# A tenth place for a piece of expert weights, and the spill branch ahead of the last scatter

## The chip, the cores and the metric

The kernel runs on one core of a Trainium2 chip. The metric is device microseconds for one execution; before the change three runs gave 1014.17, 1015.07 and 1015.34 us, a median of 1015.07. TensorE is called PE, VectorE DVE, ScalarE ACT, GpSimd POOL and SyncE SP, as in the profile.

## The reference

Two transformer blocks follow each other on 256 tokens of width 1024, all in float32. Only the end of the first and the start of the second matter here: a mixture of 32 experts (two of them per token, each a SwiGLU with three matrices of 2 MB), a norm with the gain `norm_final`, and then the second block's projections.

```python
def hierarchical_moe(h, w_rg, b_rg, w_re, b_re, w_gate, w_up, w_down):
    ...
    def expert_rows(args):
        xb, e = args
        g = xb @ w_gate[e]
        u = xb @ w_up[e]
        return (jax.nn.silu(g) * u) @ w_down[e]
    ...
# the end of first_block, then the start of second_block
x = x + hierarchical_moe(rms_norm(x, norm_ffn[l]), ...)
return rms_norm(x, norm_final)
...
u = rms_norm_2(h, norm_mix_pre[layer])
u = moba_attention(u, attn_w_qkv[j], attn_w_o[j])
```

## The kernel before, in words

**The ring.** SBUF holds a ring of nine places (`RING`), each a piece of 2 MB: one of the matrices gate, up or down of one expert. Expert n (counted from 0) has the three places from `slots_of(n)` = (6 + 3n) mod 9 on, so expert n takes the places of expert n-3. In the first block the same memory holds other weights; experts 0 and 1 are loaded while that block ends (L592 to L600), and expert 2's three pieces as soon as it has ended.

**The loads.** SP alone issues the weights, in the order of its program, on one queue. `expert_loads` (L1650) first waits until PE has done `gate_up` of expert n-3 and issues gate and up, then waits for `down` of expert n-3 and issues down. Expert 3 has its own form, `expert_three` (L1719): its gate and up come in four quarters each, as expert 0's are used up, and its down piece after `down` of expert 0.

**The steps.** For each expert PE does `gate_up` (L1519, 32 matmuls), the turn of the hidden rows (L1530) and `down` (L1541, 16 matmuls); between them stand gathers of the next three experts' tokens (L1493), and after every second expert the scatter of a pair (L1552). ACT makes the silu and the high part of the result (L1584), DVE the product and the low part (L1644). Each expert has 64 slots for tokens. Experts 1 to 6 are written out, the rest run in a hardware loop of six experts per round, and expert 31's step stands behind it (L1803).

**After the loop.** SP waits for `gate_up` and `down` of expert 29 and issues the first six units of the second block's weights, 1 MB each, into places 3, 4 and 5 (L1824); after `gate_up` of expert 30 it issues the seventh and eighth, into place 6. These units are v0.0, v0.1, q0, k0, q1, k1, q2 and k2. Every engine then loads the flag that tells whether some expert has more than 64 tokens (L1833). PE does the last scatter (L1834), and only then does `nc.If(spill > 0)` (L1886, in the profile under L1817) branch over the program for such tokens, which isn't run with these inputs.

**The second block's start.** ACT takes squares of the scattered sums from PSUM (L2085). DVE waits for the last scatter and for the row `norm_final` (L2315, L2316) and multiplies the sums by it (L2234, `z_gained`); then come means, the scaled rows (L2247), PE's transposes (L484) and the first products (L433 to L435). The row was loaded long before, in the first block (L587), into `bc` ("gain_rows"), a tile of its own of 4 KB per partition; later gain rows come into the same tile.

Of the kernel before, what the change touches and what calls it, by code (L numbers as in the profile page):

```python
# [5 lines left out]
F32 = mybir.dt.float32  # L6
# [151 lines left out]
def build_program(nc, a, out):  # L158
# [41 lines left out]
    bc = nc.alloc_sbuf_tensor("gain_rows", [P, 1024], F32)  # L200
# [8 lines left out]
    spill_flag = nc.alloc_sbuf_tensor("spill_flag", [1, 1], I32)  # L209
    banks = [nc.alloc_psum_tensor(f"bank{i}", [P, 512], F32) for i in range(8)]  # L210
# [13 lines left out]
    def weight_parts(name, offset):  # L224
        return [[rounded(f"{name}_{part}{i}", UNIT, offset + (2 * i + k) * TILE)
                 for k, part in enumerate(("high", "low"))] for i in range(2)]

    LANE_SLOTS = (7, 0, 1, 6)
    lanes1, parts1 = pieces(*LANE_SLOTS), weight_parts("w1", slot_at(3))
    parts1.append([rounded("w1_high2", UNIT, arena_at + 4 * TILE), rounded("w1_low2", UNIT, LOW1)])  # L230
    lanes2, parts2 = pieces(3, 4, 5, 6), weight_parts("w2", slot_at(0))
# [331 lines left out]
    def first_sync():  # L563
# [22 lines left out]
        SP.wait_ge(*vgain.at(1))  # L586
        load_row("norm_final", a["norm_final"].rearrange("(l n) -> l n", l=1))  # L587
# [945 lines left out]
    def down(q, n, w, odd):  # L1533
# [3 lines left out]
        wd = ring[:, w * PIECE:(w + 1) * PIECE].rearrange("p (c n) -> p c n", n=D)  # L1537
# [8 lines left out]
    def scatter(q, y_made, turned_, b, h, signal):  # L1546
# [3 lines left out]
        for t in range(JT):  # L1550
            for y in Y[t]:
                last = PE.matmul(ACC[2 * h + t][:, :], ROUTET[:, b, t, h, :], y[:, :], start=False, stop=True,  # L1552
                                 skip_group_check=True)
        if signal:
            last.then_inc(*q.inc("scattered"))
# [94 lines left out]
    def expert_loads(q, e, n, w, w_dn, sems, gate_up_read=None):  # L1650
        if gate_up_read is not None:
            SP.wait_ge(*q.at("gate_up", gate_up_read))
        for i, src in enumerate((w_gate, w_up)):
            SP.dma_start(ring[:, (w + i) * PIECE:(w + i + 1) * PIECE],
                         src[bass.ds(e, 1), :, :].rearrange("o p n -> (o p) n")).then_inc(sems[i], 16)
        SP.wait_ge(*q.at("down", n))
        SP.dma_start(ring[:, w_dn * PIECE:(w_dn + 1) * PIECE],
                     w_down[bass.ds(e, 1), :, :].rearrange("o p n -> (o p) n")).then_inc(sems[2], 16)

    def slots_of(n):  # L1660
        return (6 + 3 * n) % RING
# [162 lines left out]
    for u in order2[0:6]:  # L1824
        load_second(u)
# [620 lines left out]
```

## Time and profile before

| | |
|---|---|
| median of the three runs | 1015.07 us |
| the profiled execution's own time | 1013.95 us |
| its span | 1012.7 us |
| mean granted clock of TensorE | 0.986 |
| DMA traffic | 289.66 MB, of which the experts' weights 201 MB |
| PE, DVE, ACT busy | 94%, 44%, 36% |

The span is shown on the page as 40 slices of 25.3 us each. The experts run in slices 10 to 28, from some 243 to 701 us. Times in the trace are us from the start of the span. In the view of the chain that ended last, "issue" is time for which the profile shows no releaser; in the DMA view, the last number of an issue is the time from its issue on SP to its landing.

### The profile page before, as it was taken

What the parts mean: (1) busy time and instruction counts of PE and PEld (TensorE: products, weight loads), DVE (VectorE), ACT (ScalarE), POOL (GpSimd) and SP (SyncE); (2) the same over time, 40 slices, a digit from 0 to 9 for tenths busy, and PEclk for the clock granted to TensorE, in tenths of its full rate; (3) what the DMA queues carried; (4) which work ended last, traced back from release to release, by engine and by line L of the source; (5) the groups of instructions that cost most, each with busy time, mean ns of one, the idle gap of its engine ahead of it and who ended that gap; (6) DMA issues with size and microseconds to landing.
All of it is one profiled execution on the core that took longest, in us unless ns stands there. A gap on an engine that the chain in (4) does not pass through costs nothing.

```text
span 1012.7 us, 13539 instructions
## 1 busy us (share of the span) xinstructions
PE 956.6 (94%) x5353; PEld 653.8 (65%) x5353; DVE 441.1 (44%) x757; ACT 360.3 (36%) x593; POOL 26.2 (3%) x40
## 2 busy tenths in 40 slices
PE   6999989998999999999999999985999989999997
PEld 5979878985444444444444444332998879998886
DVE  5856555445232232222222222214564755555434
ACT  7635446433121121111111112114455544554332
POOL 1400000000000000000000000000000000000000
PEclk9989999998999999999999999999999989999999
DMA  9943443486899999999999999999645535555501
GB/s 319 361 146 126 167 164 134 161 316 264 311 430 421 429 428 426 427 429 428 429 428 430 428 428 428 428 428 362 212 156 165 167 107 164 180 192 172 205 1 42
DMA packets 72629, 289.66 MB, mean 286 GB/s; under 512 B 4993, under 2 KB 44545, under 8 KB 60546
## 3 DMA queue, kind: packets, MB, share of 16 engines
q1 hardware_dynamic: 72002, 288.79, 73.8%
q8 instruction: 35, 0.57, 0.2%
q10 hardware_dynamic: 576, 0.17, 0.1%
q14 instruction: 16, 0.13, 0.0%
HBM read 287.90 MB, written 1.05 MB: 285 GB/s over the span
## 4 chain that ended last, share of the span: by engine, by line
PE 79%; issue 6%; ACT 6%; DVE 5%; DMA 4%; POOL 1%; SPq 0%; ACTq 0%; DVEq 0%
PE bank L1519 21%; PE bank L433 11%; PE bank L434 11%; PE bank L435 11%; PE bank L1541 10%; PE bank L1493 4%; DMA ring<-in_w_up 3%; ACT w_high L494 3%; PE bank L1552 3%; DVE w_low L523 1%; DVE arena L2303 1%; PE bank L1530 1%; ACT hidden_high L2127 1%; PE bank L723 1%; PE bank L761 1%
## 5 line engine op out<-in xcount | busy, mean ns | idle before, releaser
L1519 PE MATMUL bank<-ring,arena 128*64 128x512 f32 x1024 | 228.7, 598 | 7.9 <-issue 7.1
L523 DVE TENSOR_TENSOR w_low<-ring,w_high 128x2048 fp32r<-128x2048 f32 x76 | 174.1, 2290 | 122.3 <-ACT w_high L494 122.3
L494 ACT ACTIVATE w_high<-ring 128x2048 fp32r<-128x2048 f32 x76 | 145.1, 1909 | 120.8 <-PE bank L435 120.7
L1519 PEld LDWEIGHTS bank<-ring,arena 128*64 128x64 f32 x1024 | 75.5, 137 | 140.9 <-issue 139.0
L1541 PE MATMUL bank<-ring,arena 128*64 128x512 f32 x512 | 116.9, 597 | 5.3 <-issue 5.3
L433 PE MATMUL bank<-xT_high,w_high 128*128 128x256 f32 x384 | 112.0, 292 | 2.6 <-DVE xT_low L532 1.8
L434 PE MATMUL bank<-xT_low,w_high 128*128 128x256 f32 x384 | 109.8, 286 | 0.0
L435 PE MATMUL bank<-xT_high,w_low 128*128 128x256 f32 x384 | 109.7, 286 | 0.0
L1644 DVE SCALAR_TENSOR_TENSOR y_low<-bank,arena,y_high 64x512 fp32r<-64x512 f32 x64 | 48.0, 750 | 139.3 <-ACT y_high L1584 138.8
L1584 ACT ACTIVATE y_high<-bank,arena 64x512 fp32r<-64x512 f32 x64 | 43.7, 683 | 135.3 <-PE bank L1541 134.9
L1571 ACT ACTIVATE arena<-bank 128x256 f32<-128x256 f32 x32 | 12.3, 385 | 191.1 <-PE bank L1519 191.1
L1541 PEld LDWEIGHTS bank<-ring,arena 128*64 128x64 f32 x512 | 37.4, 136 | 63.3 <-issue 63.3
L433 PEld LDWEIGHTS bank<-xT_high,w_high 128*128 128x128 f32 x384 | 74.8, 195 | 4.4 <-issue 2.0
L1638 DVE TENSOR_TENSOR arena<-bank,arena 128x256 f32<-128x256 f32 x32 | 13.6, 424 | 146.2 <-ACT arena L1571 146.2
L434 PEld LDWEIGHTS bank<-xT_low,w_high 128*128 128x128 f32 x384 | 74.8, 195 | 0.1
L435 PEld LDWEIGHTS bank<-xT_high,w_low 128*128 128x128 f32 x384 | 74.8, 195 | 0.0
L1493 PEld LDWEIGHTS bank<-onehot,rows_high 128*128 128x128 f32 x176 | 34.6, 197 | 31.7 <-issue 31.5
L433 PE MATMUL bank<-w_high,hidden_high 128*128 128x512 f32 x128 | 50.0, 391 | 0.7 <-DVE arena L2303 0.5
L435 PE MATMUL bank<-w_high,hidden_low 128*128 128x512 f32 x128 | 49.8, 389 | 0.0
L434 PE MATMUL bank<-w_low,hidden_high 128*128 128x512 f32 x128 | 49.8, 389 | 0.0
L1493 PE MATMUL bank<-onehot,rows_high 128*128 128x192 f32 x176 | 46.0, 298 | 1.0 <-DVE onehot L1593 1.0
L1493 PE MATMUL bank<-onehot,rows_low 128*128 128x192 f32 x176 | 43.0, 280 | 0.0
(280 smaller groups left out, 1455.9 us busy)
## 6 DMA issues: line engine op xcount, KB each, us to landing
ring<-in_w_down SPq DMA_DIRECT2D x32, 2048.0 KB, 25.0
ring<-in_w_gate SPq DMA_DIRECT2D x31, 2048.0 KB, 21.3
ring<-in_w_up SPq DMA_DIRECT2D x31, 2048.0 KB, 25.8
ring<-in_w_up SPq DMA_DIRECT2D x16, 1024.0 KB, 5.6
ring<-in_w_down SPq DMA_DIRECT2D x16, 1024.0 KB, 5.0
ring<-in_attn_w_qkv SPq DMA_DIRECT2D x12, 1024.0 KB, 11.8
ring<-in_w_in SPq DMA_DIRECT2D x10, 1024.0 KB, 11.7
ring<-in_w_kv_mem SPq DMA_DIRECT2D x8, 1024.0 KB, 5.2
```

What stands on the lines that cost most here:

```text
L433: PE.matmul(o, lh, rh, start=start, stop=False, skip_group_check=True)
L434: PE.matmul(o, lh, rl, start=False, stop=False, skip_group_check=True)
L435: return PE.matmul(o, ll, rh, start=False, stop=stop, skip_group_check=True)
L494: SC.activation(parts[buffer[0][u]][0][:, :], lanes[n % len(lanes)], ACT.Copy).then_inc(*high.inc(u))
L523: DVE.tensor_tensor(p[1][:, :], lanes[n % len(lanes)], p[0][:, :].bitcast(F32), ALU.subtract).then_inc(*split.inc(u))
L1493: last = PE.matmul(bank[:, c * width:(c + 1) * width], part[:, h, k * P:(k + 1) * P], ONEHOT[buffer][:, h, 0:width], start=h == 0 and part ...
L1519: last = PE.matmul(GU[t * SLOTS:(t + 1) * SLOTS, 0:NGU], xs[:, k, :], wgu[:, :, k, t * (DE // JT):(t + 1) * (DE // JT)], start=k == 0, sto ...
L1541: last = PE.matmul(DN[t * SLOTS:(t + 1) * SLOTS, 0:NY], HT[:, o:o + SLOTS], wd[:, k, (t ^ odd) * NY:((t ^ odd) + 1) * NY], start=k == 0, s ...
L1552: last = PE.matmul(ACC[2 * h + t][:, :], ROUTET[:, b, t, h, :], y[:, :], start=False, stop=True, skip_group_check=True)
L1584: last = SC.activation(Y[t][0][p, :], DN[p, 0:NY], ACT.Copy, scale=SLOT_WEIGHT[p, b, t:t + 1])
L1638: DVE.tensor_tensor(HID, GU[:, DE // JT:NGU], SILU, ALU.mult).then_inc(*q.inc("hidden"))
L1644: last = DVE.scalar_tensor_tensor(out=Y[t][1][p, :], in0=DN[p, 0:NY], scalar=SLOT_WEIGHT[p, b, t:t + 1], in1=Y[t][0][p, :].bitcast(F32), o ...
```

## The change

A tenth place, `extra`, is allocated; its first 4 KB per partition are the tile `bc`, which has no memory of its own any more. Only one piece goes there: expert 3's down. It needs no place of expert 0 and is issued right after the quarters of gate and up. From expert 4 on all places are lower by one: expert 4 has up in place 8 (where expert 0's down was), gate in 1 and down in 0; expert 5 has 2, 3, 4; expert 6 has 5, 6, 7; expert 7 again 1, 8, 0. So in experts 4 to 6 one piece is issued after `down` of expert n-4 and the two others after `gate_up` of expert n-3. From expert 7 on each takes the places of expert n-3 and waits as before.

`norm_final` can't stay in `bc` while expert 3's down is there. Its load moves from the first block to behind the sixth unit of the second block's weights. Of those units four are issued after expert 29 (places 3 and 4), and the fifth and sixth, the row, the seventh and eighth after `gate_up` of expert 30.

The branch over the program for spilled tokens now stands ahead of the last scatter; inside it, the scatter is done once more and the rows are cleared after. The memory reserved for dynamic DMA is set to 2048 bytes per partition.

```diff
-    bc = nc.alloc_sbuf_tensor("gain_rows", [P, 1024], F32)
+    extra = nc.alloc_sbuf_tensor("extra_piece", [P, PIECE], F32)
+    bc = extra[:, 0:1024]
...
-    lanes2, parts2 = pieces(3, 4, 5, 6), weight_parts("w2", slot_at(0))
+    lanes2, parts2 = pieces(3, 4, 5, 6), weight_parts("w2", slot_at(1), slot_at(0))
...
         for u in order1[4:29]:
             load_first(u)
-        SP.wait_ge(*vgain.at(1))
-        load_row("norm_final", a["norm_final"].rearrange("(l n) -> l n", l=1))
         load_first(order1[29])
...
-    def gate_up(q, n, w, buffer, e, chunks_=range(KC)):
+    def gate_up(q, n, gate, up, buffer, e, chunks_=range(KC)):
-        wgu = ring[:, w * PIECE:(w + 2) * PIECE].rearrange("p (m c n) -> p m c n", m=2, c=KC)
+        wgu = ring[:, :].rearrange("p (s c n) -> p s c n", s=RING, c=KC)[:, gate:up + 1:up - gate, :, :]
...
+    def expert_loads(q, n, n0):
+        gate, up, dn = places_of(n0)
+        SP.wait_ge(*q.at("gate_up", n - 2))
+        if up < gate + 2:
+            load_piece(gate, expert_of(w_gate, n), place_sem[gate])
+            load_piece(up, expert_of(w_up, n), place_sem[up])
+        else:
+            load_piece(up, expert_of(w_up, n), place_sem[up])
+            load_piece(gate, expert_of(w_gate, n), place_sem[gate])
+        SP.wait_ge(*q.at("down", n - 2))
+        load_piece(dn, expert_of(w_down, n), place_sem[dn])
+
+    def places_of(n):
+        if n < 4:
+            w = (6 + 3 * n) % RING
+            return w, w + 1, EXTRA if n == 3 else w + 2
+        w = (5 + 3 * n) % RING
+        return (1, w, 0) if w + 1 == RING else (w, w + 1, w + 2)
...
+    def early_loads(n):
+        gate, up, dn = places_of(n)
+        if n == 2:
...
+        elif n == 3:
+            for part in range(4):
+                if part < 3:
+                    SP.wait_ge(quarters, part + 1)
+                else:
+                    SP.wait_ge(*q.at("gate_up", 1))
                 o = slice(part * PIECE // 4, (part + 1) * PIECE // 4)
+                SP.dma_start(piece(gate)[:, o], w_gate[n][:, o]).then_inc(place_sem[gate], 16)
+                SP.dma_start(piece(up)[:, o], w_up[n][:, o]).then_inc(place_sem[up], 16)
+            SP.wait_ge(*vgain.at(1))
+            load_piece(dn, w_down[n], place_sem[dn])
+        else:
+            first, second = ((gate, w_gate), (up, w_up)) if gate < up < gate + 2 else ((up, w_up), (gate, w_gate))
+            SP.wait_ge(*q.at("down", n - 3))
+            load_piece(first[0], first[1][n], place_sem[first[0]])
+            SP.wait_ge(*q.at("gate_up", n - 2))
+            load_piece(second[0], second[1][n], place_sem[second[0]])
+            load_piece(dn, w_down[n], place_sem[dn])
...
-    for u in order2[0:6]:
+    for u in order2[0:4]:
         load_second(u)
     SP.wait_ge(*q.at("gate_up", NE - 1))
+    for u in order2[4:6]:
+        load_second(u)
+    load_row("norm_final", a["norm_final"].rearrange("(l n) -> l n", l=1))
     for u in order2[6:8]:
         load_second(u)
...
     spill = nc.values_load(spill_flag[0:1, 0:1], min_val=0, max_val=1)
-    scatter(q, NE, NE, LAST % 3, 0, False)
-    scatter(q, NE, NE, LAST % 3, 1, True)
...
     with nc.If(spill > 0):
+        scatter(q, NE, NE, LAST % 3, 0, False)
+        scatter(q, NE, NE, LAST % 3, 1, False, last_pair_scattered)
...
+        for t in range(JT):
+            for y in Y[t]:
+                DVE.memset(y[:, :].bitcast(F32), 0.0).then_inc(rows_cleared, 1)
+        PE.wait_ge(rows_cleared, 2 * JT)
+    scatter(q, NE, NE, LAST % 3, 0, False)
+    scatter(q, NE, NE, LAST % 3, 1, True)
...
-    nc = bacc.Bacc("TRN2", target_bir_lowering=False, num_devices=1)
+    nc = bacc.Bacc("TRN2", target_bir_lowering=False, num_devices=1, dynamic_dma_scratch_size=2048)
```

## Rows read from the trace of the kernel before

**Rows 1.** The page: PE over the span; DMA busy tenths and GB/s of 40 slices

```profile
PE 956.6 (94%) x5353; PEld 653.8 (65%) x5353; DVE 441.1 (44%) x757; ACT 360.3 (36%) x593; POOL 26.2 (3%) x40
...
DMA  9943443486899999999999999999645535555501
GB/s 319 361 146 126 167 164 134 161 316 264 311 430 421 429 428 426 427 429 428 429 428 430 428 428 428 428 428 362 212 156 165 167 107 164 180 192 172 205 1 42
```

**Rows 2.** Chain that ended last, 681 to 703 us: start, us, what

```profile
681.65 1.39 issue
683.05 7.10 PE bank L1519 x32
...
692.03 3.67 PE bank L1541 x16
...
698.70 2.13 PE bank L1552 x8
...
701.68 1.30 DVE arena L2234 x2
```

**Rows 3.** Timeline of SP: gate loads released by gate_up of experts 7, 19, 25

```profile
354.45 0.33 SPq L1654 DMA_DIRECT2D ring<-in_w_gate  x1
...
518.51 0.33 SPq L1654 DMA_DIRECT2D ring<-in_w_gate  x1
...
602.66 0.33 SPq L1654 DMA_DIRECT2D ring<-in_w_gate  x1
```

**Rows 4.** Stretches: last three columns are PE clock, DMA share, GB/s

```profile
264.50:267.00 2.50, 2.50 (x16) 1.27 (x16) 1.29 (x2) 1.88 (x4) 0.00 (x0) 1.00 0.66 177
...
271.00:274.50 3.50, 3.20 (x22) 1.77 (x20) 1.49 (x4) 0.77 (x2) 0.00 (x0) 1.00 0.44 89
275.00:480.00 205.00, 202.89 (x1004) 89.65 (x1000) 54.55 (x116) 39.37 (x80) 0.00 (x0) 1.00 1.01 427
```

**Rows 5.** Timeline of SP: expert 3's down, expert 4's gate, expert 7's gate

```profile
264.28 0.33 SPq L1730 DMA_DIRECT2D ring<-in_w_down  x1
272.37 0.33 SPq L1654 DMA_DIRECT2D ring<-in_w_gate  x1
...
313.50 0.33 SPq L1654 DMA_DIRECT2D ring<-in_w_gate  x1
```

**Rows 6.** DMA view, us to landing: the issues of 264.28 and of 313.50

```profile
ring<-in_w_down SPq DMA_DIRECT2D x1, 2048.0 KB, 7.8
...
ring<-in_w_gate SPq DMA_DIRECT2D x1, 2048.0 KB, 12.1
```

**Rows 7.** Timeline of SP: expert 31's up, units k1 and q3, a later gain row

```profile
646.78 0.38 SPq L1654 DMA_DIRECT2D ring<-in_w_up  x1
...
693.48 2.92 SPq L1819 DMA_DIRECT2D ring<-in_attn_w_qkv  x1
...
703.33 1.83 SPq L1819 DMA_DIRECT2D ring<-in_attn_w_qkv  x1
...
708.46 0.34 SPq L561 DMA_DIRECT2D gain_rows<-in_norm_mix_post  x1
```

**Rows 8.** DMA view, us to landing: the four issues of rows 7, in order

```profile
ring<-in_w_up SPq DMA_DIRECT2D x1, 2048.0 KB, 36.2
...
ring<-in_attn_w_qkv SPq DMA_DIRECT2D x1, 1024.0 KB, 11.7
...
ring<-in_attn_w_qkv SPq DMA_DIRECT2D x1, 1024.0 KB, 10.7
...
gain_rows<-in_norm_mix_post SPq DMA_DIRECT2D x1, 512.0 KB, 6.8
```

**Rows 9.** Flag load and branch on PE's queue: ns min/median/max, first and last start

```profile
L1833 PEldq TENSOR_LOAD <-spill_flag x1: 483/483/483, 692.1 to 692.1; - x1
...
L1817 PEldq COMPARE_BRANCH  x1: 6243/6243/6243, 698.8 to 698.8; - x1
```

**Rows 10.** Timeline of PE: the first transposes of the second block

```profile
706.22 1.97 PE L484 MATMUL bank<-ident,arena 128*128 128x128 f32 x8 [5.41 <-DVE arena L2247]
```

More of the change, by code:

```diff
@@ L1646, in y_low_out, with load_piece, expert_of, landed @@
         last.then_inc(*q.inc("y"))
[L1650 to L1661, printed above, removed]
+    def load_piece(place, src, sem):
+        SP.dma_start(piece(place), src).then_inc(sem, 16)
+    def expert_of(src, e):
+        return src[bass.ds(e, 1), :, :].rearrange("o p n -> (o p) n")
+    def expert_loads(q, n, n0):
[9 more added lines that the diff above has]
+        load_piece(dn, expert_of(w_down, n), place_sem[dn])
+    EXTRA = RING
+    def places_of(n):
[4 more added lines that the diff above has]
+        return (1, w, 0) if w + 1 == RING else (w, w + 1, w + 2)
+    LOADS_OF = {3: 4}
+    def landed(n):
+        return [16 * sum((LOADS_OF.get(m, 1) if part < 2 else 1) for m in range(n + 1) for part, p in enumerate(places_of(m))
+                         if p == place) for place in places_of(n)]
+    def piece(place):
+        return extra[:, :] if place == EXTRA else ring[:, place * PIECE:(place + 1) * PIECE]
     q = Handoffs(nc, "moe_")
@@ L1667, in tensor_step @@
     def tensor_step(n, n0, i, trio, pair, more=True):
-        w, s, buffer, b, odd = slots_of(n0), n0 % TRIO, n0 // TRIO % 2, n0 // 2 % 3, n0 % 2
+        s, buffer, b, odd = n0 % TRIO, n0 // TRIO % 2, n0 // 2 % 3, n0 % 2
         p = PIECES_AT.get(n0 % 6) if more else None
+        if i is None:
+            known, later = n0, 0
+        else:
+            known, later = n0 + 2 * TRIO, i - 1
+        gate, up, dn = places_of(known)
+        value_gate, value_up, value_dn = landed(known)
         if p is not None:
             gather_even(q, trio + 1, p, 1 - buffer)
-        for part in (0, 1):
-            PE.wait_ge(slot_sem[w + part], 16 * (n0 // 3 + 1) + 32 * i + (48 if n0 % 3 == 0 and n0 else 0))
+        for place, value in ((gate, value_gate), (up, value_up)):
+            PE.wait_ge(place_sem[place], value + 32 * later)
         PE.wait_ge(*q.at("xT_even", 2 * trio + 2))
@@ L1678, in tensor_step @@
         PE.wait_ge(*q.at("routeT", n + 1))
-        gate_up(q, n, w, buffer, s)
+        gate_up(q, n, gate, up, buffer, s)
         if odd and p is not None:
@@ L1690, in tensor_step @@
             turn_route(q, n + 1, (b + odd) % 3, 1 - odd, pair + odd + 1, GU)
-        PE.wait_ge(slot_sem[w + 2], 16 * (n0 // 3 + 1) + 32 * i)
-        down(q, n, w + 2, odd)
+        PE.wait_ge(place_sem[dn], value_dn + 32 * later)
+        down(q, n, piece(dn), odd)
     def scalar_step(n, n0, trio, pair):
@@ L1756, in tensor_begin @@
         turn_route(q, 1, 0, 1, 1, GU)
-        PE.wait_ge(slot_sem[w + 2], 16)
-        down(q, 0, w + 2, 0)
+        PE.wait_ge(place_sem[dn], 16)
+        down(q, 0, piece(dn), 0)
     def scalar_begin():
```

67 lines of the change are left out of this document (33 added, 34 removed).

## The prediction

> **What bounds the kernel now.** I read the page first. PE is busy for 94% of the span, but the DMA row of the slices stands at nine tenths or more, with 421 to 430 GB/s, from slice 11 to slice 26, which is nearly the whole of the experts [rows 1]. So two limits lie close together there, and the question is which one ends last at expert 31.
>
> The pace of PE alone can be read off SP's timeline, since each gate load is released by the end of a `gate_up`. From `gate_up` of expert 7 to that of expert 19 it is 518.51 - 354.45 = 164.06 us for twelve experts, 13.67 each. One expert's 3 x 2048 KB at 427 GB/s need 14.7 us [rows 3, 4]. DMA is the slower one, by 1.0 us for each expert; the ring begins with a lead, and PE lives on it. From expert 19 to 25 the time is 84.15 us, 2.1 more than six times 13.67: here the lead is used up. By PE's own pace `gate_up` of expert 31 would end at 518.51 + 164.06 = 682.57; it ended at 683.05 + 7.10 = 690.15 [rows 2, 3]. So 7.6 us of PE's time in the last dozen experts is waiting for weights. The last such wait is plain: expert 31's up piece landed at 646.78 + 36.2 = 682.98, and the matmuls began at 683.05 [rows 2, 7, 8]. What is gained here is thus whatever brings the whole stream of weights to its end earlier, up to 7.6 us.
>
> **What the tenth place gives.** I then looked for idle time of the DMA queue at the start of the stream. From 264.5 to 267 us it moved 177 GB/s and from 271 to 274.5 us 89 GB/s, while from 275 us on the mean is 427 [rows 4]. The missing bytes are 2.5 x (427 - 177) + 3.5 x (427 - 89) = 1808 KB, 4.2 us of the full rate. They are missing because expert 3's down waits for `down` of expert 0 (264.28) and expert 4's gate and up for `gate_up` of expert 1 (272.37) [rows 5]. With the change expert 3's down goes out right behind the quarters, some 5 us earlier, and expert 4's up takes its moment at 264.28. Both holes close, and the queue is one piece ahead: 2048 KB at 427 GB/s, 4.9 us.
>
> Not all of this survives. From expert 7 on each load waits for the same `gate_up` as before, which the change can't move. A piece issued to an empty queue lands 7.8 us after its issue (expert 3's down) [rows 5, 6]. Expert 7's first piece is issued at 313.50, so it lands no sooner than 321.3. It landed at 313.50 + 12.1 = 325.6 before [rows 5, 6]. The stream is therefore at most 4.3 us ahead from there on; one piece's time, 4.9 us, would have been more, so 0.6 us is given back in a short hole at expert 7. Later the queue only grows longer (1.0 us for each expert), so nothing more is lost. The term is **-4.3 us**. The ends: 4.9 (one piece, no hole) and 0 (the lead is lost again, see the rivals). As 7.6 us of waiting were there, PE is still bound by the stream at expert 31, and its last scatter ends at 698.70 + 2.13 - 4.3 = 696.5 instead of 700.8 [rows 2].
>
> **What the row `norm_final` costs.** It was in SBUF 500 us before it was needed. Now it stands in the same queue, behind all of the experts and six units of the second block. That queue is full here, and SP's issues show it: one takes 2.92 us, about what its 1 MB needs [rows 7]. The sixth unit, k1, landed at 693.48 + 11.7 = 705.2, which is 22.2 us after expert 31's up; the last scatter ended 17.8 us after it [rows 2, 7, 8]. Both distances are made of work that the change leaves alone, so both move with the stream. The row itself I price by the later gain row of the same size: it landed at 708.46 + 6.8 = 715.3, and the 1 MB unit ahead of it at 703.33 + 10.7 = 714.0, so it takes 1.2 us more [rows 7, 8]; its upper end is a whole unit's 2.9. DVE starts about 0.1 us behind the landing. So the first multiplication starts 22.2 + 1.2 + 0.1 = 23.5 us after the landing of expert 31's up. Before, it started at 701.68, 18.7 us after it [rows 2]. The term is **+4.8 us**, with ends of 0 (the row isn't what DVE waits for) and 6.5.
>
> Queued behind this wait on DVE are the four multiplications, the means and the scaled rows, and PE's transposes wait for those [rows 10]. ACT's squares from PSUM don't need the row and go ahead, but the first square of whole rows needs the first two multiplications, so the sequence after the wait is as long as before. Behind it PE is busy nearly without a gap, so the delay reaches the end.
>
> **What the branch costs.** In the profile of before PE's branch starts at 698.8 and takes 6.24 us, and it is hidden: it ends at 705.1, and PE's next work at 706.22 waits for DVE [rows 9, 10]. The branches of the other engines aren't moved. Placed ahead of the scatter, it starts behind the flag load, at 692.1 + 0.5 = 692.6, and ends at 698.9 by the clock of before; the scatter began at 698.70 [rows 2, 9]. That is 0.2 us late, and the scatter now has over 4 us before the row lands: the cost is 0 as long as the row is late, 0.2 us if that cover is gone. Its ends are 0 and 6.2, the second less the 5 us of cover.
> The Trainium skill (Runtime: NRT & Kernel Launch, Instruction fetch mechanics) has a rule against this move: a taken branch whose target lies outside the window already fetched must fetch the target by DMA first, and the engine stalls. The trace agrees, with its 6.24 us. By the rule alone the scatter would be late by all that isn't hidden behind ACT and DVE making expert 31's rows, which is the same 0.2 us.
>
> **The small edits.** The row's load leaves the first block at 157 us, where the queue moved 134 to 167 GB/s [rows 1]: nothing waited for it, 0. `gate_up` of every third expert reads gate and up from places that lie apart instead of side by side, and up is issued first: PE has 1.0 us to spare for each expert up to expert 19, and at 31 it waits for the second piece in any order, 0. Lanes and halves of the second block's first units move to other places, each free at its time: 0. The SBUF kept for dynamic DMA is smaller: 0, since every load is issued by SP or ACT as before.
>
> **The sum.** -4.3 + 4.8 + 0 = +0.5 us, against the profiled execution's 1013.95: 1014.5. The median of the runs lies 1.1 above that execution, so I predict 1015.6 us.
>
> **The rivals.**
> *The row isn't waited for.* Then the scatter's 4.3 us reach the end, less 0.2 for the branch: 1015.07 - 4.1 = 1011.0 us. For this the row would have to land within 18.6 us of expert 31's up, ahead of two or three units that were issued before it. Against it speaks the later gain row, which landed after the unit ahead of it [rows 7, 8]. I give it 0.11.
> The Trainium skill (DMA: Bandwidth & Descriptors, Queues, rings and completion order) says that completion isn't in order of issue for one issuing engine. It would allow this rival; the row above speaks for order here.
>
> *The lead is lost again: slower.* The place is expert 7. If its first piece lands later than 321.3, the stream's gain is smaller by as much, while the row's 4.8 us stay. From a landing of 322.9 on (a gain of 2.7) the kernel is more than 2.03 us slower; with no gain it is 1015.07 + 4.8 = 1019.9 us. This is also the case in which the tenth place doesn't do what it says. For it speaks that the hole at expert 7 exists by my own numbers; against it, that the queue is full again from the next expert on. I give it 0.18, and another 0.03 to a row dearer than 2.7 us.
>
> *Neither term is as sized, but they cancel.* It is the forecast with its ends: a gain of 3.0 to 4.9 and a row at 4.8 to 5.5 give -0.1 to +2.5, mostly within 0.2%.
>
> **How the numbers follow.** A difference of 0.2%, 2.03 us, is about what a measurement of this kernel can tell from none. Faster by more: the first rival, 0.11. Slower by more: 0.21. Within: 0.68. The forecast's own range is 1014.4 to 1017.6, with 0.6 us for the spread of the medians. To hold 8 in 10 I go down to 1012.8, part of the way to the first rival, and up to 1018.6, through more than half of the second.
>
> **What would show it.** In the profile of after, expert 3's down is issued near 259.5 and expert 4's up near 264.3; the stretches from 264.5 to 274.5 are full; expert 7's first piece lands near 321.3 with its issue unmoved; expert 31's up lands near 678.7, and its `gate_up` starts at once; the branch on PE starts near 688 and takes about 6 us; the last scatter ends near 696.5; the row lands near 702.1, and DVE's first L2234 starts at 702.2 with an idle time of some 5 us before it that ends with a DMA. If L2234 follows the scatter within 1 us, my second term is wrong. If expert 31's up lands at 682 or later, the first is.

## The result, and the profile after

The changed kernel takes 1018.54 us (median of nine runs, 1017.38 to 1020.43), the kernel before 1015.34 (nine runs, 1014.17 to 1017.65). The ratio is 1.0027, with a 95% interval of 1.0015 to 1.0040: slower by 0.27%, which is 2.7 us; the two medians are 3.2 us apart. The time lies in the range given, but on the slower side of the 0.2% that separates a difference from none. The forecast was no difference.

The profiled execution of after has a time of its own of 1020.28 us and a span of 1019.0, 6.3 us above those of before. The first thing to see is that 2.0 us of this is there before the experts begin, and is no work of the change. The timeline of PE from 11.5 us on, before and then after (start, length; idle time and its releaser in brackets):

```profile
11.94 0.47 PE L433 MATMUL bank<-w_high,hT_high 128*128 128x512 f32 x1 [0.64 <-DVE w_low L1112]
...
12.48 0.39 PE L435 MATMUL bank<-w_high,hT_low 128*128 128x512 f32 x1
12.71 0.40 PE L433 MATMUL bank<-w_high,hT_high 128*128 128x512 f32 x1
```

```profile
11.80 0.77 PE L434 MATMUL bank<-w_high,hT_high 128*128 128x512 f32 x1 [0.59 <-DVE w_low L1111]
...
12.79 0.63 PE L436 MATMUL bank<-w_high,hT_low 128*128 128x512 f32 x1
13.22 0.63 PE L434 MATMUL bank<-w_high,hT_high 128*128 128x512 f32 x1
```

In before the matmuls follow each other every 0.23 us, in after every 0.43, until 16.7 us. That is the pace of the half clock (1.2 GHz), the one that the scatter further down has at a granted clock of 0.50; the trace itself has no record of after's clock ahead of 16.5 us, where it becomes 1.00. From then on PE reaches the same points 2.0 us apart up to the experts. This fits the runs, which fall in two groups, before at 1014.2 to 1015.3 and at 1016.5 to 1017.7, after at 1017.4 to 1018.8 and at 1019.8 to 1020.4; group against group after is 2.9 to 3.1 us longer. The profiled before is in the lower group and the profiled after in the upper one. So I compare the traces from a common point, the issue of expert 4's gate, which `gate_up` of expert 1 releases in both: 272.37 in before [rows 5], 274.34 in after. **From there to the start of PE's last matmul after takes 739.08 us and before 734.66: 4.4 us longer.**

The page of after (DMA tenths and GB/s of the slices, the chain's shares by engine):

```profile
DMA  9943543486999999999999999999445535555501
GB/s 320 361 141 124 166 147 116 163 321 261 380 428 398 427 425 430 428 425 431 428 427 430 425 431 430 424 423 350 155 165 165 161 109 166 169 193 177 206 1 42
...
PE 71%; DMA 12%; ACT 5%; issue 5%; DVE 5%; SPq 1%; POOL 1%; ACTq 0%; DVEq 0%
```

Against [rows 1] slice 10 has gone from 311 to 380 GB/s: the hole in front of expert 4 is filled. Slice 12, from 306 to 331 us, has gone from 421 to 398: another hole has come. The stretches show both, and a third (the last three columns are PE's clock, DMA's share and GB/s). After:

```profile
264.50:267.00 2.50, 2.50 (x15) 1.20 (x12) 0.00 (x0) 0.73 (x2) 0.00 (x0) 1.00 1.05 406
271.00:274.50 3.50, 3.50 (x18) 1.14 (x15) 0.00 (x0) 0.15 (x1) 0.00 (x0) 1.00 0.99 426
...
275.00:277.00 2.00, 1.70 (x12) 1.01 (x12) 1.48 (x4) 0.38 (x1) 0.00 (x0) 1.00 0.92 336
277.00:279.00 2.00, 2.00 (x12) 0.86 (x10) 0.00 (x0) 0.00 (x0) 0.00 (x0) 1.00 0.91 360
315.00:317.00 2.00, 2.00 (x11) 1.26 (x9) 0.42 (x1) 0.54 (x2) 0.00 (x0) 1.00 0.92 320
317.00:319.00 2.00, 2.00 (x12) 1.03 (x12) 0.75 (x2) 0.23 (x1) 0.00 (x0) 1.00 0.85 319
319.00:325.00 6.00, 6.00 (x32) 2.46 (x30) 1.95 (x3) 2.10 (x4) 0.00 (x0) 1.00 0.99 385
325.00:480.00 155.00, 153.19 (x757) 67.12 (x753) 41.59 (x92) 29.01 (x59) 0.00 (x0) 1.00 1.01 428
```

Before, around the issue of expert 7's gate:

```profile
315.00:317.00 2.00, 2.00 (x12) 1.06 (x12) 0.76 (x2) 0.26 (x1) 0.00 (x0) 1.00 0.96 410
317.00:323.00 6.00, 6.00 (x33) 2.46 (x30) 1.92 (x3) 2.10 (x4) 0.00 (x0) 1.00 1.01 429
```

The holes of 177 and 89 GB/s [rows 4] are closed. But 275 to 279 us lacks (427 - 336) x 2 + (427 - 360) x 2 = 316 KB, 0.7 us, and 315 to 325 us lacks (427 - 320) x 2 + (427 - 319) x 2 + (427 - 385) x 6 = 682 KB, 1.6 us. The issues of after on SP:

```profile
261.53 0.43 SPq L1652 DMA_DIRECT2D extra_piece<-in_w_down  x1
266.25 0.33 SPq L1652 DMA_DIRECT2D ring<-in_w_up  x1
274.34 0.33 SPq L1652 DMA_DIRECT2D ring<-in_w_gate  x1
...
315.47 0.33 SPq L1652 DMA_DIRECT2D ring<-in_w_up  x1
```

and, in the DMA view, how long the issue of 315.47 and that of the row (697.87) took to land:

```profile
ring<-in_w_up SPq DMA_DIRECT2D x1, 2048.0 KB, 10.0
...
extra_piece<-in_norm_final SPq DMA_DIRECT2D x1, 512.0 KB, 9.8
```

Expert 7's first piece landed 10.0 us after its issue, not the 7.8 of an empty queue [rows 6]. The chain that ended last shows the rest of the way:

```profile
648.13 36.23 DMA ring<-in_w_gate
684.36 0.04 issue
684.40 7.11 PE bank L1518 x32
691.51 3.45 SPq L1865
...
697.87 9.82 DMA extra_piece<-in_norm_final
...
707.78 1.30 DVE arena L2294 x2
```

It is the chain of [rows 2] up to `gate_up` of expert 31. There it leaves PE: it goes over SP, whose issues stand in line, to the row and then to DVE. On the timeline of after:

```profile
697.87 2.90 SPq L562 DMA_DIRECT2D extra_piece<-in_norm_final  x1
...
700.06 0.80 PE L1551 MATMUL bank<-y_high,routeT 128*128 128x512 f32 x1 [3.02 <-DVE y_low L1645]
...
703.21 0.63 PE L1551 MATMUL bank<-y_low,routeT 128*128 128x512 f32 x1
...
707.78 1.89 DVE L2294 TENSOR_TENSOR arena<-bank,extra_piece 128x512 f32<-128x512 f32 x3 [7.78 <-DMA extra_piece<-in_norm_final]
...
712.33 1.97 PE L485 MATMUL bank<-ident,arena 128*128 128x128 f32 x8 [8.48 <-DVE arena L2307]
```

DVE's 7.78 us of idle time end with the row. Against [rows 10] the transposes are late by 6.1 us, 4.1 of them behind the common point. There is one thing that I hadn't foreseen at all: the scatter's eight matmuls go from 700.06 to 703.84, 3.78 us where before needed 2.13 [rows 2]. The stretches of the scatter say why, after and then before (PE's clock is the third number from the end):

```profile
699.30:704.00 4.70, 3.78 (x8) 2.48 (x8) 0.70 (x1) 1.21 (x2) 0.00 (x0) 0.50 1.08 337
```

```profile
699.00:703.90 4.90, 1.82 (x8) 1.12 (x6) 2.01 (x4) 2.72 (x8) 0.00 (x0) 1.00 1.10 349
```

In after the granted clock is at 0.50 (1.2 GHz) for the whole scatter, having fallen while PE idled for y_low, in before at 1.00 (2.4 GHz). Here it cost nothing, since the row came later still.

**Where the stream's gain went.** A DMA raises its semaphore sixteen times, once for each share of it that an engine has done, and PE waits for the last. The trace has the time of each. For the second piece of expert 31, in us from the common point (the last column is the start of PE's last matmul):

```
kernel                    first share   last share   between   scatter       first transposes  last matmul
before                       408.33       410.59       2.26    426.33-428.45      433.85          734.66
row_late_only                408.23       410.78       2.55    426.61-428.72      439.92          741.33
branch_only                  408.48       411.31       2.83    427.13-430.00      435.40          736.09
before_warm                  408.30       410.66       2.36    426.40-428.53      435.23          736.00
after                        405.74       410.02       4.27    425.72-429.50      437.99          739.08
row_behind_four              405.83       409.88       4.05    425.59-429.37      434.78          735.79
row_early                    405.79       408.54       2.75    424.44-428.05      433.46          734.17
row_early_branch_back        405.94       409.26       3.31    424.96-428.65      434.05          734.89
place_kept_busy              406.00       409.50       3.49    425.21-427.34      432.75          732.88
halves                       405.95       410.04       4.09    425.75-429.53      434.94          735.88
halves_warm                  406.07       409.27       3.19    424.97-427.09      433.75          734.58
halves_row_behind_four       404.85       408.08       3.22    423.84-426.73      432.14          732.75
all_three                    404.66       407.04       2.38    422.83-424.94      431.15          731.91
```

(The kernels below after are those of the experiments.) In after the fastest share is 2.6 us earlier than in before, and the slowest, which counts, 0.6. By the slowest share after is ahead of before by 4.5 us at expert 6's down, by 2.1 at expert 7's first piece, by 1.7 at expert 8's second piece and by 0.6 at expert 8's down; from there on the 0.6 stays. So all of the loss lies between 315 and 352 us.

### The profile page after: what moved, and what is told of

Same layout as the page of the kernel before. It is cut to its first block, busy times and chain, and to the rows that moved or that the text cites. A ratio compares the mean times of both kernels' runs of the same rounds, so it can differ in the third digit from the quotient of the medians.

```text
span 1019.0 us, 13534 instructions
## 1 busy us (share of the span) xinstructions
PE 960.8 (94%) x5353; PEld 656.0 (64%) x5353; DVE 441.1 (43%) x757; ACT 360.3 (35%) x593; POOL 26.2 (3%) x40
## 4 chain that ended last, share of the span: by engine, by line
PE 71%; DMA 12%; ACT 5%; issue 5%; DVE 5%; SPq 1%; POOL 1%; ACTq 0%; DVEq 0%
PE bank L1518 18%; PE bank L434 11%; PE bank L436 11%; PE bank L435 11%; DMA ring<-in_w_gate 10%; PE bank L1540 8%; PE bank L1492 4%; ACT w_high L495 3%; PE bank L1551 2%; DVE w_low L524 1%; DVE arena L2363 1%; DMA extra_piece<-in_norm_final 1%; ACT hidden_high L2187 1%; PE bank L722 1%; PE bank L760 1%
## 5 line engine op out<-in xcount | busy, mean ns | idle before, releaser
L1518 PE MATMUL bank<-ring,arena 128*64 128x512 f32 x1024 | 228.7, 598 | 7.3 <-DMA ring<-in_w_gate 3.7
L1540 PE MATMUL bank<-ring,arena 128*64 128x512 f32 x496 | 113.3, 598 | 5.0 <-issue 5.0
## 6 DMA issues: line engine op xcount, KB each, us to landing
ring<-in_w_up SPq DMA_DIRECT2D x31, 2048.0 KB, 23.5
ring<-in_w_down SPq DMA_DIRECT2D x31, 2048.0 KB, 24.6
```

What stands on the lines that cost most here:

```text
L1518: last = PE.matmul(GU[t * SLOTS:(t + 1) * SLOTS, 0:NGU], xs[:, k, :], wgu[:, :, k, t * (DE // JT):(t + 1) * (DE // JT)], start=k == 0, sto ...
L1540: last = PE.matmul(DN[t * SLOTS:(t + 1) * SLOTS, 0:NY], HT[:, o:o + SLOTS], wd[:, k, (t ^ odd) * NY:((t ^ odd) + 1) * NY], start=k == 0, s ...
```

## The experiments

My theory after reading the two traces: the row's wait costs what I had said (4 to 5 us), the tenth place gives 2.5 us in the fastest share and less in the slowest, and the half clock at the scatter takes 1.6 us once the row is out of the way. The first rival: the row is hidden or nearly so, and something else in the new ring is slow. The second: the branch ahead of the scatter costs, by itself or by what it does to the clock.

Each ratio is against runs of the kernel before on the same chip, and a time difference that is worked out from a ratio can differ by up to 1 us from that of the medians. Their medians were 1015.27 us for the first four kernels, 1016.31 for the next four and 1016.83 for the last three; so kernels of different groups are compared by their ratios.

**1. The row alone.** The ring of before, with the row behind the sixth unit:

```diff
-        SP.wait_ge(*vgain.at(1))
-        load_row("norm_final", a["norm_final"].rearrange("(l n) -> l n", l=1))
         load_first(order1[29])
...
     SP.wait_ge(*q.at("gate_up", NE - 1))
+    SP.wait_ge(*vgain.at(1))
+    load_row("norm_final", a["norm_final"].rearrange("(l n) -> l n", l=1))
     for u in order2[6:8]:
```

> Edit: the kernel of before, with the load of norm_final alone moved behind the sixth unit of the second block's weights (k1); no tenth place, no branch moved. Theory (the row is what costs): the row lands 23.4 us after expert 31's up and DVE's first L2234 waits for it instead of for the scatter, so the kernel is 4.8 us slower than before, about 1020. Rival (the row's wait is covered or short, and the loss of the change lies in the branch or in the ring): within 1 us of before.

Measured: 1021.23 us (1019.26 to 1022.03, five runs), ratio 1.0050 [1.0032, 1.0069], so 5.1 us slower (the medians are 6.0 apart). The chain of this kernel takes the same turn as that of after:

```profile
697.35 10.88 DMA gain_rows<-in_norm_final
...
708.32 1.30 DVE arena L2234 x2
```

DVE starts 24.6 us behind the landing of expert 31's second piece (435.38 against 410.78 from the common point), 5.9 later than in before. The row's wait is shown by itself, at the size of my second term or a little above. The rival that it is hidden falls.

**2. The branch alone.** The ring and the row of before, with the branch and the second scatter as in the change:

```diff
+    last_pair_scattered = nc.alloc_semaphore("last_pair_scattered")
     with nc.If(spill > 0):
+        scatter(q, NE, NE, LAST % 3, 0, False)
+        scatter(q, NE, NE, LAST % 3, 1, False, last_pair_scattered)
...
+    scatter(q, NE, NE, LAST % 3, 0, False)
+    scatter(q, NE, NE, LAST % 3, 1, True)
```

> Edit: the kernel of before, with the branch over the spill program alone moved ahead of the last scatter. Theory (the branch is covered): the branch starts right behind the flag load near 692.7 and ends within 6.3 us, the scatter starts 0 to 0.2 us later, time within 0.5 us of before. Rival (the branch is what costs, by its fetch or by a scatter at half clock): the scatter starts or ends 1.5 us or more later and the kernel is 1.5 to 3 us slower than before.

Measured: 1015.83 us (eleven runs), ratio 1.0006 [0.9996, 1.0016]: no difference, though a cost of up to 1.6 us isn't excluded. PE's branch ran from 695.58 for 5.82 us, to 701.40; the scatter, released by y_low, began at 701.64. It took 2.86 us, part of it at the half clock, and ended 1.55 us later after the common point than in before. That is the size that the rival had named for a late scatter; some 0.7 of it is there at the landing of expert 31's second piece already, and some 0.7 is the clock. In the change itself the branch is shorter (in the column of the line's instructions: its length, three times, in ns, and its start):

```profile
L1547 PEldq COMPARE_BRANCH  x1: 4539/4539/4539, 694.0 to 694.0; - x1
```

It ended at 698.6, and the scatter began at 700.06, released by y_low. In the thirteen kernels the branch took between 4.54 and 7.98 us. The Trainium skill (Runtime: NRT & Kernel Launch, Instruction fetch mechanics) says that a taken branch out of the window already fetched stalls until its target has been fetched; these lengths agree. In nine kernels the branch was wholly covered and in row_early all but 0.2 us of it; in the other three it wasn't, as experiments 7, 8 and 11 show.

**3. The row early.** The change, with the row between the loads of experts 6 and 7, as soon as expert 3's down has been used:

```diff
             if first:
+                if j == 5:
+                    SP.wait_ge(*q.at("down", 4))
+                    load_row("norm_final", a["norm_final"].rearrange("(l n) -> l n", l=1))
                 early_loads(2 + j) if j < 5 else expert_loads(q, 7, 7)
...
-    load_row("norm_final", a["norm_final"].rearrange("(l n) -> l n", l=1))
     for u in order2[6:8]:
```

> Edit: the kernel of after, with the load of norm_final moved to between the loads of expert 6 and of expert 7, behind down of expert 3, where the DMA queue of after has a hole. Theory (row costs 4.8, the stream of weights gains only 0.6 in after): DVE's first multiplication follows the scatter again, 4.2 us or more faster than after, so 0.6 to 1.5 us faster than before, about 1014; expert 31's last weights land as in after. Rival (the stream does gain the 4.3 us I forecast, and the trace of after was one bad execution): 4 us faster than before, about 1011.

Measured: 1015.10 us (eleven runs), ratio 1.0001 [0.9991, 1.0011]. With the row's wait gone the kernel is 2.6 us faster than the change (1.0027), yet no faster than before. The expectation, 4.2 us or more faster than the change, was a miss. Its scatter begins 1.9 us earlier than before's and takes 3.61 us instead of 2.12, so it ends only 0.4 earlier: the half clock, which the row's wait had hidden, takes 1.5 us back. The branch ended at 696.94, 0.1 us behind y_low (696.85), and the scatter began at 697.11, 0.2 later than in the kernels where it follows y_low.

**4. The row early and the branch back.** On top of 3:

```diff
+    scatter(q, NE, NE, LAST % 3, 0, False)
+    scatter(q, NE, NE, LAST % 3, 1, True)
...
     with nc.If(spill > 0):
-        scatter(q, NE, NE, LAST % 3, 0, False)
-        scatter(q, NE, NE, LAST % 3, 1, False, last_pair_scattered)
```

> Edit: as row_early, and the branch over the spill program stands behind the last scatter again, as before. It is the tenth place alone, without the cost of the row. Theory (the branch is covered in either place): within 0.5 us of row_early. Rival (the branch ahead of the scatter costs): 1.5 us or more faster than row_early.

Measured: 1014.50 us (eleven runs), ratio 0.9990 [0.9981, 0.9999]. Its interval overlaps that of 3; the ratios are 1.1 us apart, between the 0.5 of the theory and the 1.5 of the rival, while in the two profiles 3 is 0.7 us the faster. The scatter takes 3.69 us here too. So the half clock at the scatter comes without the branch ahead of it as well. The second rival, at 1.5 us or more, falls; a smaller cost of the branch isn't excluded by the runs, and the traces show only the 0.2 of experiment 3.

**5. The row two units earlier.** The change, with the row behind the fourth unit:

```diff
     for u in order2[0:4]:
         load_second(u)
+    load_row("norm_final", a["norm_final"].rearrange("(l n) -> l n", l=1))
     SP.wait_ge(*q.at("gate_up", NE - 1))
     for u in order2[4:6]:
         load_second(u)
-    load_row("norm_final", a["norm_final"].rearrange("(l n) -> l n", l=1))
```

> Edit: the kernel of after, with the load of norm_final behind the fourth unit of the second block's weights instead of behind the sixth. Theory (the row lands in the order of issue, each unit ahead of it costs 3.0 us): it lands 6 us earlier, before the last scatter ends, DVE doesn't wait for it, and the kernel is 3 to 4.3 us faster than after, about 1015. Rival (the wait is a fixed price of a row loaded in this crowded stretch, wherever it stands): within 1 us of after, 1018 to 1019.

Measured: 1015.11 us (ten runs), ratio 0.9986 [0.9972, 0.9999]. The row lands 427.33 us from the common point, 2.0 before the scatter's end, and the chain goes over the scatter again:

```profile
698.47 3.80 PE bank L1551 x8
...
703.12 1.30 DVE arena L2294 x2
```

The change's 1.0027 has become 0.9986 (on another chip), 4.2 us, by moving one load of 4 KB per partition past two units. That is the cost of where the row was put.

**6. Expert 7 in halves.** To close the hole at expert 7 (and for one expert in each later round of six), gate and up are issued in two halves each, the first when PE has used half of expert 4's. The row is early and the branch back, as in 4:

```diff
+            if half and k == KC // 2 - 1:
+                last.then_inc(halfway, 1)
...
+        if in_halves(n0):
+            SP.wait_ge(halfway, n - 3)
+            for o in (slice(0, UNIT), slice(UNIT, PIECE)):
+                if o.start:
+                    SP.wait_ge(*q.at("gate_up", n - 2))
+                for place, w in (((gate, w_gate), (up, w_up)) if up < gate + 2 else ((up, w_up), (gate, w_gate))):
+                    SP.dma_start(piece(place)[:, o], expert_of(w, n)[:, o]).then_inc(place_sem[place], 16)
```

> Edit: the tenth place with the row early and the branch back in its old place (row_early_branch_back), and for expert 7 and for the first load of each round of the loop (experts 8, 14, 20, 26) gate and up come in two halves, the first issued when gate_up of expert n-3 is half done, some 3.5 us earlier. Theory (the lead of one piece is lost at expert 7, because its loads can't be issued before gate_up of expert 4): the hole of the queue near 316 us closes, the last weights of expert 31 land 2 to 2.7 us earlier against gate_up of expert 1 than in row_early_branch_back, and the kernel is some 2 us faster than it, 1012.5. Rival (the lead is lost in another way, by transfers that are slowed or by the code's own fetches): less than 0.5 us.

Measured: 1015.02 us (eleven runs), ratio 0.9987 [0.9972, 1.0001], as in 4. I had expected the last share of expert 31's second piece 2 to 2.7 us earlier than in 4 (409.26); it came 0.8 later (410.04), and the fastest at the same 405.95. A miss. SP's issues show the reason:

```profile
306.80 0.33 SPq L562 DMA_DIRECT2D extra_piece<-in_norm_final  x1
310.23 0.33 SPq L1673 DMA_DIRECT2D ring<-in_w_up  x1
...
313.66 0.33 SPq L1673 DMA_DIRECT2D ring<-in_w_up  x1
```

The halves went out 3.4 us before the rest. But the row stood ahead of them and took 1.1 us of the queue (405.95 here against 404.85 in experiment 10). In 3 it stands in the hole and costs nothing (405.79 against 405.74 in after).

**7 and 8. PE kept at work ahead of the scatter.** Twelve transposes whose results nobody uses stand behind expert 31's step, and twenty more behind the scatter. 7 is 6 with them, 8 the kernel before with them:

```diff
     tensor_step(NE - 1, NE - 1, None, (NE - 1) // TRIO, LAST, more=False)
+    for _ in range(12):
+        PE.transpose(GATH[:, 0:P], ident[:, :], ident[:, :])
...
     scatter(q, NE, NE, LAST % 3, 1, True)
+    for _ in range(20):
+        PE.transpose(GATH[:, 0:P], ident[:, :], ident[:, :])
```

> Edit: as halves, and PE does 12 transposes of the identity into a bank that is not in use behind expert 31's down, and 20 behind the last scatter, where it stands idle for 3.0 and 5.4 us. The results are not used. Theory (the granted clock falls to half in these idle times and costs 1.6 us at the scatter in some executions and 1.8 us at the second block's first transposes): at full clock the scatter takes 2.1 us instead of 3.7 and each row of eight transposes 1.0 instead of 1.9, and the kernel is 2 to 4 us faster than halves. Rival (the added matmuls delay the scatter or the first transposes by as much): within 0.5 us of halves or slower.

> Edit: the kernel of before with the same 12 and 20 transposes of the identity, and nothing else. Theory (the half clock behind the experts is a cost of before as well): 1.5 to 3 us faster than before. Rival (it costs only in the changed kernels): within 0.5 us of before.

Measured: 7 has 1016.07 us (eleven runs), ratio 0.9992 [0.9979, 1.0005], 8 has 1015.70 (eleven runs), 0.9999 [0.9984, 1.0014]. Both expectations, 2 to 4 and 1.5 to 3 us faster, were misses. In 7 the scatter takes 2.12 us again, where 6 needed 3.78: the twelve do what they are for. The twenty do harm: the second block's first transposes follow the scatter's end by 6.7 us in both kernels instead of 5.4, and 1.3 of the 1.6 us is given back. In 8, whose scatter was at full clock anyway, nothing is gained. The harm comes by way of the branch, which stands behind the twenty on PE. In 8:

```profile
700.77 2.35 PE L1839 MATMUL bank<-ident 128*128 128x128 f32 x20
...
L1819 PEldq COMPARE_BRANCH  x1: 6568/6568/6568, 701.0 to 701.0; - x1
...
707.63 2.61 PE L484 MATMUL bank<-ident,arena 128*128 128x128 f32 x11 [4.52 <-issue]
```

It begins at 701.01, 2.2 us later than in before, and ends at 707.58; the transposes start 0.05 us behind its end. In 7 it ends at 708.33 and they start at 708.38. A branch that was covered in before no longer is. Two edits in one kernel was a poor choice here; only the table above takes them apart.

**9. The place and the twelve.** 4 with the twelve transposes and not the twenty:

```diff
     tensor_step(NE - 1, NE - 1, None, (NE - 1) // TRIO, LAST, more=False)
+    for _ in range(12):
+        PE.transpose(GATH[:, 0:P], ident[:, :], ident[:, :])
     silu_out(q, NE - 1)
```

> Edit: as row_early_branch_back, and PE does the 12 transposes of the identity behind expert 31's down, but none behind the last scatter. Theory (in the kernels with the tenth place the scatter ran at half clock, 3.6 to 3.8 us instead of 2.1, and this hides the gain of the stream; the 20 transposes behind the scatter are what delayed halves_warm): the scatter takes 2.1 us, the first transposes of the second block start 5.4 us behind its end, and the kernel is 1.5 us faster than row_early_branch_back, 2 to 2.5 us faster than before. Rival: within 0.5 us of row_early_branch_back, 1 us faster than before.

Measured: 1012.62 us (1011.37 to 1014.95, six runs), ratio 0.9960 [0.9944, 0.9975]. In its chain the scatter is short:

```profile
700.13 2.15 PE bank L1551 x8
```

Against 4 (measured on another chip) the ratio falls by 0.30%, 3.0 us, more than the 1.5 expected; the two profiles give 2.0 (732.88 against 734.89), of which 1.6 is the scatter.

**10. Halves, the row behind four.** 6, with the row as in 5:

```diff
-                if j == 5:
-                    SP.wait_ge(*q.at("down", 4))
-                    load_row("norm_final", a["norm_final"].rearrange("(l n) -> l n", l=1))
...
     for u in order2[0:4]:
         load_second(u)
+    load_row("norm_final", a["norm_final"].rearrange("(l n) -> l n", l=1))
```

> Edit: as halves, but the row norm_final stands behind the fourth unit of the second block's weights instead of ahead of expert 7. Theory (in halves the row took the time of the hole that the halves closed, 1.3 us): the first of the sixteen shares of expert 31's second piece is done 404.4 to 405.0 us behind the issue of expert 4's gate, where row_early, row_behind_four and halves have 405.8 to 406.0 and before has 408.3; the time 1 us under halves. Rival (the lead is bounded by something else than the hole at expert 7): 405.8 to 406.0 again and the same time as halves.

Measured: 1013.88 us (twelve runs), ratio 0.9974 [0.9963, 0.9985]. The fastest share is at 404.85 us, 1.1 earlier than in 6 and 3.5 earlier than in before. Seven kernels with the place and either the hole or the row in it have 405.74 to 406.07; only without both does it move. Where it moves is shown by the fastest shares on the way: in after they are 4.4 us ahead of before at expert 6's down and 2.5 at expert 7's, here 4.1 and 4.0 (3.5 at expert 31). So expert 7 is where the stream's gain was capped, though the same edit changes one expert's loads in each later round too.

**11. All three.** 10 with the twelve transposes:

```diff
     tensor_step(NE - 1, NE - 1, None, (NE - 1) // TRIO, LAST, more=False)
+    for _ in range(12):
+        PE.transpose(GATH[:, 0:P], ident[:, :], ident[:, :])
```

> Edit: as halves_row_behind_four, with the 12 transposes of the identity behind expert 31's down. Theory: both gains add, 1012 to 1013 us where before has 1015.3, so 2.5 to 3.5 us faster than before. Rival: no more than the 1 us that row_early_branch_back had.

Measured: 1012.07 us (1011.48 to 1013.70, six runs), ratio 0.9959 [0.9946, 0.9973]: 0.41% faster than before, 4.2 us, where I had expected 2.5 to 3.5; 0.7% faster than the change.

```profile
695.55 2.12 PE bank L1555 x8
...
698.53 1.30 DVE arena L2308 x2
```

The chain goes over the scatter without a wait for the row (landed 424.71 us from the common point, the scatter's end is at 424.94). By the medians it can't be told from 9, which is simpler; by the profiles it is 1.0 us ahead. It could be more, for the branch, back behind the scatter, isn't covered here:

```profile
L1886 PEldq COMPARE_BRANCH  x1: 7979/7979/7979, 695.8 to 695.8; - x1
...
703.88 2.40 PE L485 MATMUL bank<-ident,arena 128*128 128x128 f32 x10 [6.21 <-DVE arena L2321]
```

It ends at 703.82, and the transposes follow the scatter's end by 6.2 us instead of 5.4. The branch ahead of the scatter, as the change has it, might save these 0.8 us; no run has it together with the twelve transposes.

## Why the prediction was right or wrong

**The stream term, -4.3 us, failed.** It came out at -0.6 in the profiled after, and at -1.4 as a mean: the last share of expert 31's second piece stands at 409.44 us in the five kernels with the tenth place and without halves, at 410.84 in the four with the old ring. The step that failed is the price of expert 7's first piece. I took 7.8 us from expert 3's down and so allowed a loss of 0.6; it took 10.0 to land, and the lead of the slowest share fell by 2.4 there. The 7.8 belonged to a queue that was just running empty and whose engines were close together: expert 3's down was issued at 264.28, and the sixteen shares of the piece ahead of it were done between 263.73 and 264.86. At expert 7 in after those of the piece ahead were done between 316.04 and 318.23. Two things were wrong with the step.

First, the holes. Expert 7's piece was issued at 315.47; the fastest share of the piece ahead was done at 316.04 and its own at 322.73, 6.7 us later, where 4.9 is the full pace. An issue 0.6 us ahead of the end didn't keep the queue full. My estimate is that the next bytes come some 2 us after their issue: 0.6 + 1.6 here, 1.3 + 0.7 at expert 4, and in before, where expert 3's down met an almost empty queue, its fastest share was done 6.8 us after the issue, 1.9 more than the full pace. It cost 1.6 us by the stretches, and the same thing at expert 4's gate (issued 1.3 us ahead of the end of the piece before it, at 275.65) 0.7, which I had not put in the sum. One piece less these, 4.9 - 0.7 - 1.6 = 2.6 us, is what the fastest share shows: 408.34 as a mean of the four kernels with the old ring, 405.86 of the five with the place, 2.5 us. Experiment 10 shows that expert 7 caps it.

Second, the spread. I had treated the queue as one stream with one end. It has sixteen, and PE waits for the latest. Behind the stretches in which the old ring leaves the queue empty they are close together: expert 4's gate has 0.96 us between its first and last share, in after 2.4 (in experiment 1 the last quarter ahead of the first such stretch has 2.1 and the piece behind it 1.1). At expert 31 it is 2.5 as a mean in the four kernels and 3.6 in the five, which is the other 1.1 us. So a part of what the old holes cost wasn't lost.

What pushes one share back is seen in the moments: a 16 KB instruction fetch at 347.66 in after falls together with a rise from 3.0 to 4.2 us between two pieces that follow each other. All thirteen traces bear this out. Between 286 and 690 us the distance changes by more than 0.2 us from one piece to the next 42 times, 30 times up and 12 down, and each time the last share comes within 7.5 us behind the start of a fetch, where only 170 of the 1119 pieces lie. Most fetches change nothing, 71 of 117, that of 346.86 in before among them. Of the kernels with the place and without halves, after, 5 and 9 have a rise of 1.2 to 1.5 us at the fetch near 348, and 3 and 4 have none there: the first three end 0.6 to 1.1 us ahead of before, the other two 2.1 and 1.3. That the fetch causes it isn't shown, since fetches weren't moved or taken away, and what decides which fetch does it stays open.

**The row's term, +4.8 us, was right.** DVE starts 23.4 us behind the landing of expert 31's second piece (707.78 - 684.36), and I had said 23.5. Against 18.7 before this is 4.7. By the ratios it is 5.1 (experiment 1) and 4.2 (after against experiment 5), though only 2.6 against experiment 3, where the half clock takes the wait's place. The landing stayed in the order of issue: the row landed at 707.69 and the unit ahead of it at 706.33, 1.4 us apart, where I had put 1.2. So the first rival, that the row is not waited for, was wrong for this kernel, and moving the row by two units made it true.

**The branch, 0, was right** in after: what I had weighed against it, the stall of a taken branch, is 4.5 us there and ends 1.5 us ahead of the scatter's start. Alone it is 1.0006, with an interval that reaches to 1.6 us, and the 0.2 us that I had put for a branch without the row's cover are what the trace of experiment 3 has. The start I named, 688, was too early by about as much as the stream was (694.0, which is 692.0 on the time scale of before).

**The small edits, 0.** Nothing in the trace speaks against it; they weren't tried alone.

**The rival that won is "the lead is lost again"**, with its place and its point: expert 7, and a landing later than 322.9. It landed at 325.51, which is 323.5 on the time scale of before. I gave it 0.18. The landing that I had named as the mark of a wrong first term, expert 31's second piece at 682 or later, came true as well: 684.36, 682.4 on that scale. In the profiled pair the sum with what was measured is -0.6 + 4.7 = +4.1 us, which is the lateness of the transposes; with the stream's mean, -1.4 + 4.7 = +3.3, it is close to the 3.2 of the medians. "Within 0.2%" failed by 1.2 us by the medians and by 0.7 by the ratio, and it failed because a term was mis-sized, not because one was missing: the one I didn't foresee, the half clock at the scatter, was hidden under the row. That the time still lies in the range, by 0.1 us, is owed to the width that I gave it toward this rival.

It is an unforeseen term of the kernels without that wait, though. Had the row been free, my 1011.0 us would not have come: 5 stands at 0.9986 and 3 at 1.0001, since the stream gives 1.4 us instead of 4.3 and 1.5 to 1.6 us of half clock take the place of the wait. Together with the twelve transposes the place does give 0.4%.

## What to carry to other kernels

Price the piece that opens a hole by its issue against the end of the piece ahead of it, since an issue less than about 2 us ahead leaves a hole, and count an added place only down to the next load that it can't bring forward. A small row needed at a stage's start belongs ahead of big units in a full queue or into a hole, where it costs nothing; measure each edit against the wait that will take its place. Work that is put in front of a covered branch takes its cover away. Look at the last share of a transfer, not at the mean rate of the queue.

## What the runs showed of the hardware

The sixteen shares of a 2 MB load drift apart under a full queue, from 1.0 to 2.3 us in before and from 1.1 to 4.3 in after. Between 286 and 690 us the steps fall together with instruction fetches; most lead apart, some closer (from 2.1 to 1.2 us at 312 us in experiment 9). From 425 to 680 us, where there is no fetch, the distance stays within 0.1 us in twelve of the thirteen kernels and within 0.2 in the other. The Trainium skill (DMA: Bandwidth & Descriptors, Why a DMA increments its semaphore by 16 and not by 1) says that a DMA's engines finish independently and that only the full count means landed; the trace agrees, and adds that the distance is worth as much as most edits here.

PE's granted clock fell to 0.50 some 2.1 us into an idle time of 3.0 us ahead of the scatter in after, and not in the same 3.0 us in before (in before it fell at 704.0, 3 us behind the scatter). It was at the half for all or part of the scatter in every kernel with the tenth place and no added transposes, in part in experiment 2, and never with the twelve transposes. What in the time ahead decides it was not found.

The traced executions begin at the pace of either clock: matmuls 0.23 or 0.43 us apart from 11.8 to 16.7 us, worth 2.0 us at the common point (eight kernels at 272.4 to 272.9, five at 274.3 to 274.9). In before and after this fits the two groups of runs. It isn't the whole of the spread: the traced execution of experiment 1 began at the pace of the full clock and lies among its slower runs all the same (1021.23).
